# Issuing the experts' down-weight loads from ScalarE's queue instead of SyncE's

## The reference

```
for layer in range(2):
    h = rms_norm(x, norm1_w[layer]);  x = x + hybrid_mixer(h, ...)
    h = rms_norm(x, norm2_w[layer])
    x = x + (swiglu(h, ...) if layer == 0 else moe_swiglu(h, ...))

def moe_swiglu(h, w_router, b_router, w_gate, w_up, w_down):   # 8 experts, d_ff 3584, top 2
    gates = softmax over the two largest of (h @ w_router + b_router), 0 elsewhere
    for e in range(8):
        a = silu(h @ w_gate[e]) * (h @ w_up[e])                # [256, 3584]
        out = out + gates[:, e] * (a @ w_down[e])              # [256, 1024]
```

## Time and profile before

| | |
|---|---|
| median of three timed runs | 1741.08 us (1740.41 to 1741.96) |
| profiled execution | 1742.23 us, of which its span 1740.5 us |
| PE busy | 1730.2 us, 99% of the span |
| DVE busy | 1382.5 us, 79% |
| ACT busy | 1101.2 us, 63% |
| DMA queue of SP | 216096 packets, 483.44 MB, 75.4% of 16 engines' span |
| moved over the span | 498.41 MB, mean 286 GB/s |
| loads of gate, up and down weights of the experts | 112 each, 1024 KB each, median 7.2, 7.6 and 7.2 us from issue to landing |

### The profile page before, as it was taken

One profiled execution on the slowest core, in us unless ns is written; L12 is line 12 of the kernel. 1 busy time (PEld: TensorE's weight loads), 2 busy tenths in 40 slices (PEclk: granted clock), 3 DMA queues, 4 the chain that ended last, 5 costly groups with the idle time before them and its releaser, 6 DMA issues.

```text
span 1740.5 us, 22783 instructions
## 1 busy us (share of the span) xinstructions
PE 1730.2 (99%) x8390; PEld 1448.9 (83%) x8390; DVE 1382.5 (79%) x1140; ACT 1101.2 (63%) x976; POOL 119.8 (7%) x123
## 2 busy tenths in 40 slices
PE   8999999999999999999999999999999999999998
PEld 8888888888888888898888888888888888888887
DVE  7966587555578665868888889889888888898898
ACT  4455574444343566637777777777777777777775
POOL 1021000000000210007100000000000000000100
PEclk9999999999999999989999999999999999999999
DMA  8555365554545434658999999999999999999995
GB/s 315 193 167 166 121 237 222 190 187 130 172 170 191 166 94 145 217 218 287 402 351 412 382 359 411 372 368 400 351 400 393 348 412 375 363 411 367 371 413 203
DMA packets 219848, 498.41 MB, mean 286 GB/s; under 512 B 8296, under 2 KB 13168, under 8 KB 219632
## 3 DMA queue, kind: packets, MB, share of 16 engines
q1 hardware_dynamic: 216096, 483.44, 75.4%
q0 software_dynamic: 3696, 14.18, 2.2%
HBM read 491.80 MB, written 7.88 MB: 287 GB/s over the span
## 4 chain that ended last, share of the span: by engine, by line
PE 96%; ACT 1%; DVE 1%; DMA 0%; issue 0%; POOL 0%; SPq 0%; DVEq 0%; POOLq 0%
PE ps L741 30%; PE ps L743 30%; PE ps L742 30%; PE ps L750 4%; PE ps L746 3%; ACT sb_w L1404 0%; DVE sb_wlo L369 0%; ACT sb_whi L362 0%; DMA sb_x<-in_x_dram 0%; ACT sb_ahi L1461 0%; DVE sb_z L1782 0%; ACT L1404 0%; DVE sb_w L1673 0%; DVE sb_wlo L398 0%; ACT sb_hhi L1318 0%
## 5 line engine op out<-in xcount | busy, mean ns | idle before, releaser
L398 DVE TENSOR_TENSOR sb_wlo<-sb_z,sb_whi 128x2048 fp32r<-128x2048 f32 x334 | 756.5, 2290 | 95.2 <-ACT sb_whi L392 94.5
L392 ACT ACTIVATE sb_whi<-sb_z 128x2048 fp32r<-128x2048 f32 x333 | 634.8, 1927 | 169.2 <-PE ps L743 163.5
L741 PE MATMUL ps<-sb_whi,sb_hhi 128*128 128x512 f32 (+1 forms) x1752 | 684.6, 391 | 0.9 <-issue 0.6
L743 PE MATMUL ps<-sb_wlo,sb_hhi 128*128 128x512 f32 (+1 forms) x1752 | 676.4, 386 | 0.0
L742 PE MATMUL ps<-sb_whi,sb_hlo 128*128 128x512 f32 (+1 forms) x1752 | 676.2, 386 | 0.0
L741 PEld LDWEIGHTS ps<-sb_whi,sb_hhi 128*128 128x128 f32 x1752 | 329.6, 188 | 67.1 <-issue 3.9
L743 PEld LDWEIGHTS ps<-sb_wlo,sb_hhi 128*128 128x128 f32 x1752 | 329.3, 188 | 66.5
L742 PEld LDWEIGHTS ps<-sb_whi,sb_hlo 128*128 128x128 f32 x1752 | 329.7, 188 | 63.1
L369 DVE TENSOR_TENSOR sb_wlo<-sb_z,sb_whi 128x2048 fp32r<-128x2048 f32 (+1 forms) x74 | 158.4, 2145 | 82.7 <-ACT sb_whi L362 82.4
L362 ACT ACTIVATE sb_whi<-sb_z 128x2048 fp32r<-128x2048 f32 (+1 forms) x75 | 135.4, 1807 | 138.3 <-PE ps L743 137.7
L741 PE MATMUL ps<-sb_whi,sb_ahi 128*128 128x512 f32 x560 | 219.3, 392 | 0.0
(11 more groups left out here) (272 smaller groups left out, 1033.6 us busy)
## 6 DMA issues: line engine op xcount, KB each, us to landing
sb_z<-in_moe_w_gate_dram SPq DMA_DIRECT2D x112, 1024.0 KB, 7.2
sb_z<-in_moe_w_up_dram SPq DMA_DIRECT2D x112, 1024.0 KB, 7.6
sb_z<-in_moe_w_down_dram SPq DMA_DIRECT2D x112, 1024.0 KB, 7.2
sb_ringa<-in_w_in_dram SPq DMA_DIRECT2D x43, 1024.0 KB, 5.0
sb_z<-in_w_in_dram SPq DMA_DIRECT2D x24, 1024.0 KB, 5.6
sb_z<-in_ffn_w_up_dram SPq DMA_DIRECT2D x10, 1024.0 KB, 5.1
sb_z<-in_ffn_w_gate_dram SPq DMA_DIRECT2D x10, 1024.0 KB, 5.0
sb_z<-in_ffn_w_down_dram SPq DMA_DIRECT2D x10, 1024.0 KB, 5.0
```

Source lines behind the costliest of these rows:

```text
L392: nc.scalar.activation(e_lane(s)[0], ringb[:, s % RING_B, :], ACT.Copy).then_inc(hi_done, 1)
L398: nc.vector.tensor_tensor(lo, ringb[:, s % RING_B, :], hi.bitcast(F32), ALU.subtract).then_inc(split, 1)
L741: nc.tensor.matmul(out, lh, rh, start=start, stop=False)
L743: return nc.tensor.matmul(out, lh, rl, start=False, stop=stop)
```

## The change

The 112 loads of down weights are issued by ACT, by a new function `load_down`; SP's program keeps the loads of gate and up weights. A load has the same source, the same buffer, the same size and the same wait (`wait_split`) as before. In ACT's program it stands right behind the high part of the slot four before it: `load_down(8)` behind `e_hi_of(4)`, `load_down(20)` behind `e_hi_of(16)`. Only slots 40 and 41 both stand behind `e_hi_of(37)`. ACT's `item` gets the expert as a second argument, which ACT reads from `eid` at the start of each item after the first.

```diff
-                        def from_d(h, f0):
-                            return wd[bass.ds(f0 + h * (C // 2), C // 2), :].rearrange("(k p) n -> p k n", p=P)
...
                         with sp.Fori(0, E_CHUNKS - 1) as i:
                             for s in range(4):
                                 load(1, "B", 4 + s, from_gu(s, bass.ds(i * C + C, C)), r=i + j * E_CHUNKS)
-                            for h in range(2):
-                                load(1, "B", 8 + h, from_d(h, i * C + e * FE), r=i + j * E_CHUNKS, k=2)
-                        for h in range(2):
-                            load(1, "B", E_SLOTS - 2 + h, from_d(h, e * FE + (E_CHUNKS - 1) * C),
-                                 r=j * E_CHUNKS, k=2)
...
+                def load_down(s, f0, r):
+
+                    wait_split(act, 1, "B", s, r)
+                    act.dma_start(ringb[:, s % RING_B, :].rearrange("p (k n) -> p k n", k=2),
+                                  down_rows[bass.ds(f0 + s % 2 * (C // 2), C // 2), :].rearrange(
+                                      "(k p) n -> p k n", p=P)).then_inc(raw_b[s % RING_B], 16)
...
                     e_hi_of(act, 4, n0)
+                    load_down(8, f0, n0)
                     e_silu(1, n0, n0)
                     e_hi_of(act, 5, n0)
+                    load_down(9, f0, n0)
...
+                    def e_pair(c, i):
+
+                        s, r = E_HEAD + c * ROUND, i * 2 + n0
+                        e_round(s, i * 2 + n0 + 2 + c, r)
+                        for k in range(6, 10):
+                            e_hi_of(act, s + k, r)
+                            if k < 8:
+                                load_down(s + k + 4, i * (2 * C) + f0 + (2 + c) * C, r)
...
+                    for h in range(2):
+                        load_down(E_SLOTS - 2 + h, f0 + (E_CHUNKS - 1) * C, n0)
                     s = E_SLOTS - 8
                     e_round(s, n0 + (E_CHUNKS - 1), n0)
...
-                    item(j + 1)
+                    item(j + 1, act.value_load(eid[0:1, bass.ds(j + 1, 1)], min_val=0, max_val=NE - 1))
```

More of the change, by code:

```diff
@@ L511, in _ @@
                     gu = [a[n][0].rearrange("e d f -> (e d) f") for n in ("moe_w_gate", "moe_w_up")]
-                    wd = a["moe_w_down"][0].rearrange("e f d -> (e f) d")
                     def load_round(e, j):
@@ L1594, in e_round, with item @@
                     e_hi_of(act, s + 5, r)
-                def item(j):
+                down_rows = a["moe_w_down"][0].rearrange("e f d -> (e f) d")
+                def load_down(s, f0, r):
[3 more added lines that the diff above has]
+                                      "(k p) n -> p k n", p=P)).then_inc(raw_b[s % RING_B], 16)
+                def item(j, e):
                     n0 = j * E_CHUNKS
+                    f0 = e * FE
                     e_hi_of(act, 4, n0)
+                    load_down(8, f0, n0)
                     e_silu(1, n0, n0)
                     e_hi_of(act, 5, n0)
+                    load_down(9, f0, n0)
                     e_hi_of(act, 6, n0)
@@ L1606, in item @@
                         e_hi_of(act, s, n0)
+                        if s < E_HEAD + 2:
+                            load_down(s + 4, f0 + C, n0)
+                    def e_pair(c, i):
[5 more added lines that the diff above has]
+                                load_down(s + k + 4, i * (2 * C) + f0 + (2 + c) * C, r)
                     if isinstance(j, int):
                         for c in range(2):
[L1609 to L1612, removed]
+                            e_pair(c, 0)
                         act.wait_ge(spread_t, 1)
@@ L1616, in item @@
                         for c in range(2):
[L1617 to L1620, removed]
+                            e_pair(c, i)
+                    for h in range(2):
+                        load_down(E_SLOTS - 2 + h, f0 + (E_CHUNKS - 1) * C, n0)
                     s = E_SLOTS - 8
@@ L1638, in _ @@
                 e_hi_of(act, 3, 0)
-                item(0)
+                item(0, 0)
                 act.wait_ge(route_ok, 1)
```

## The result

The changed kernel takes 1744.47 us in the median of 11 runs (1743.63 to 1746.49); the kernel before, on the same chip, 1740.25 us in 11 runs (1738.92 to 1743.21). The ratio is 1.0027 with a 95% interval from 1.0019 to 1.0036: 4.2 us slower, a little more than the 0.2% that the prediction took for its bound. The forecast was 1741.5 us in a range from 1739.3 to 1749.0. The profiled execution took 1746.35 us with a span of 1744.6 us, 4.1 us above the span of before.

What follows compares the result with a forecast made beforehand. PE was taken to bound the experts' part at 118.43 us an item. Terms 0 (SP) + 0 (issues) + 0 (wait) + 0.4 (order) on the median of 1741.08 gave 1741.5 us, range 1739.3 to 1749.

Steps and rivals of the forecast that it cites:

- the first rival: Last item: shared engines starve a gate slot, PE waits 3.3 us, 1744.4 us; single case within 0.81, several items 0.05.
- What bounds the kernel: Experts' part: PE sets the step, 118.43 us an item; SP idles waiting for DVE, so removing its issues is worth 0.
- ACT's issues at 0: 112 issues on ACT, 0.45 us each, run beside the arithmetic: 0; upper end, all on PE's path, 50 us.
- The added wait at 0: ACT's wait for DVE's low part two slots before is over when ACT comes to it: 0.
- Loads starting later: Down loads of slots 32 and 33 start about 1.6 and 0.3 us later, with time to spare: 0.
- Queue order at 0.4 us: Last item, slots 12 and 13: down loads on their own queue make PE wait 0 to 3.3 us; 0.4 taken.
- Two queues share about evenly: From landings around POOL's gathers: 5.1 to 5.7 us a megabyte instead of 2.54, with no rate lost together.
- The waits for loads all fall in the last item: Waits for loads fall behind the last item's gathers; elsewhere loads have some microseconds in hand.
- Rate was not lost: Rival: engines change badly between 2 KB and 4 KB rows; at 365 GB/s +18 us, 1759 us; chance 0.06.
- the issue did not hold up ACT: Rival: each issue on ACT takes 1.24 us or more, arithmetic drained first; +14 us (1755 us) or +56 us; chance 0.05.
- nothing was gained: Rival, faster: PE hardly waits, so at most 0.9 us could come from waits; chance 0.03.
- no change: Whole kernel: up to 3.5 us (0.2%) either way, a single 3.3 us starving included; chance 0.81.

Runs made afterwards that it cites:

- experiment 2: Kernel before, all loads still on SP, with only ACT's added waits for DVE's low parts and reads of the expert's number: 1739.44 us, ratio 0.9999.
- experiment 1: Kernel before, down loads still on SP but each waiting for the low part of slot s - 5 instead of s - 6: 1740.73 us, ratio 1.0008.
- experiment 10: The changed kernel run once more, nothing altered: 1746.36 us in 5 runs, ratio 1.0038 to the kernel before.
- experiment 6: Changed kernel with all four gathers of the last item held until PE is done with slot 24: 1744.19 us, ratio 1.0031 to the kernel before.
- experiment 7: Changed kernel with down loads as 512 rows by 512 columns (2 KB rows), sums another function's: 1744.63 us, ratio 1.0034 to the kernel before.
- experiment 9: Changed kernel with each down load one high part later on ACT's queue (slot 41 unchanged): 1742.06 us, ratio 1.0015 to the kernel before.

## Why the prediction was right, and where it was short

The measured time lies in the range because its upper end had room for the first rival, not because the sum came out: the sum has 0.4 us for the change, and 4.2 were measured.

- *What bounds the kernel*: right. PE sets the step, 118.43 us an item before and after, and SP's issues and waits were worth nothing.
- *ACT's issues at 0*: right. 0.38 us each, beside the high parts; the upper end of 50 us never came near.
- *The added wait at 0*: right, and measured alone (experiment 2).
- *Loads starting later*: for slot 32 forecast 975.3, seen 974.64 in an execution some 0.8 us ahead of that of before, so 975.5 on its clock. Right, and free (experiment 1).
- *Queue order at 0.4 us*: the mis-sized term. It named the place and the chain (slot 13 of the last item, behind the gathers), and the size at its upper end, 3.3 us, was near the 3.1 us that PE lost at slots 12 and 13 in the first profile (3.0 in experiment 10). Slot 13 was 4.7 us late for the 5.1 worked out. But 0.4 was chosen because a later issue was thought to keep the down loads off the engines until slots 12 and 13 were in. They were issued at 1637.5 and 1640.3, when those two were outstanding, and took two thirds of the bytes from 1641.1 us on, while slot 12 landed at 1644.4 and slot 13 at 1649.96.
- *"Two queues share about evenly"*: wrong, and read from the wrong neighbour. It holds by packets, not by bytes. The spacing of landings in the earlier trace rows mixes stretches with and without gathers. The kernel before had the true share in its queue rows of 1634 to 1638 us (packets, MB, share), where POOL's gathers (q0) run against SP's gate loads:

```profile
q0 software_dynamic: 294, 1.08, 65.8%
q1 hardware_dynamic: 295, 0.59, 38.0%
```

  Packet for packet, 2 to 1 in bytes. A view of this kind before the prediction would have given SP a third of the rate against 4 KB rows, not half. The price at the upper end held all the same, as both down loads were in before slot 13, and then their bytes count and not the shares.
- *The waits for loads all fall in the last item, elsewhere some microseconds are in hand*: true of the kernel before, but not kept by the change. Seven of ACT's nine waits for loads, 22.1 of 28.2 us, are in items 0, 1 and 6, up to 4.6 us each, and one cost PE 1.05 us. The prediction had no term for an up load that comes late away from the gathers.
- *What the wait costs*: the price had no term for the clock. In the first profile and in experiment 6 1.7 us came on top of the wait, in experiments 7 and 10 nothing.
- *The rivals*: the first one, "the shared engines starve a gate slot", came true at 1744.4 against 1744.47 measured. That nearness is partly luck: its 3.3 us were added to the first median of before, 1741.08, not 1740.25, and in the profiled execution the lower clock and item 0 made up what was missing. Rate was not lost (376 GB/s over the part), the issue did not hold up ACT, and nothing was gained.
- *The chances*: this single starving was put inside "no change", as 3.3 is under 3.5 us. At 4.2 us the outcome lies at that line or just over it. A chance of its own above the line would have been the better account.
- *ACT's waits for loads*: 5 to 15 us forecast, 28.2 in the first profile, 19.9 in the second.

## What to carry to other kernels

When loads move from one queue to two, ask not what rate is lost but what order: two open queues shared by packet here, so loads needed later could overtake those needed now. Look for the one place with the least lead, here behind a burst of gathers, and count the lead of each load there, on both queues. A load put on its own queue should not be issued long before its turn: issued one slot later, so that its packets moved only after slot 12 had landed, it gave back 4.3 of 6.6 us. Later still was not tried. And look at the landings in every round, not only in the tightest place: ACT waited up to 4.6 us for up loads in items where it had waited for none before.

## What the runs showed of the hardware

- Two hardware queues took packets one for one (421 to 422 with rows of 4 and 2 KB, 821 to 820 with 2 KB both), which gave 1.66 to 0.85 MB and 1.65 to 1.62 MB, as long as both had work on all engines. The up load of slot 37 of item 0 took 14.7 us to land although the engines were not full at its end: from 880 to 882 us they moved 99 GB/s.
- Under full load the packets of a down load began to move 3.2 to 3.6 us after its issue on ACT (first profile: issued 1637.5, first packets at 1641.1; experiment 9: issued 1638.3, first packets at 1641.5).
- A DMA issue on ACT took 0.38 us in its queue and ran beside a high part in progress.
- After 2.9 us without a matmul PE once ran for 3.4 us at the lower granted clock (1.2 GHz), and after 2.6 us in experiment 6 too; after a gap of 3.1 us in the second profile of the changed kernel and of 2.3 us in experiment 7 it kept 2.4 GHz. The length of the gap alone does not tell, and what does was not looked for.
